# Attention with scaled, transposed probability rows, and the output weights loaded during it

## The chip, the cores and the metric

The kernel runs on one core of one Trainium2 chip. The metric is the device time in microseconds (us) from start to end of one execution; the median of three executions is compared. The engines are TensorE (PE; its weight loads are PEld), VectorE (DVE), ScalarE (ACT), GpSimd (POOL) and SyncE (SP), which here only issues DMAs.

## What is computed

One decoder layer on 1,024 tokens of width 1,024, everything in float32. The parts that matter here:

```
h = rmsnorm(x) * (1 + sc1) + sh1;  z = h @ w_in      # u, v, q, six k/v sets, gates
y_gm  = gelu(u) * (causal chunk mix of rmsnorm(gelu(v)) + b)
kc = gelu(flat(blocks(k_c) + pe_k) @ w1_k) @ w2_k    # 63 compressed keys; vc alike
for each head and branch b in (compressed, selected, window):
    s_b = q @ keys_b * scale - slope * distance;  p_b = masked_softmax(s_b)
    y += gate_b * (p_b @ values_b)
x = x + gt1 * (concat(y_gm, y_nsa) @ w_out)
h2 = rmsnorm(x) * (1 + sc2) + sh2
x = x + gt2 * moe(h2)        # top 4 of 32 experts;  out = rmsnorm(x)
```

There are 8 query heads of 64 dimensions in 2 key/value groups. A group's heads sit in one half of the 128 partitions, so a pair of heads (one of each group) is worked on side by side. With 16 blocks of 64 and the top 16 selected, the selected branch is full causal attention. The window is 512 keys.

## The kernel before

The program has five stages, one after the other; each ends when all engines have finished it, and the buffers of one stage are laid over those of an earlier one.

1. `project_tokens` (0 to about 375 us): the modulation vector and all projections, tile by tile of 128 tokens. The U and V weights are in `w_uv` (4 MB). When the last tile has used them, the first-layer compression weights (4 MB) are loaded into the same place (`s_cmpw`).
2. `attend` (375 to 871 us). First the compression: `compress` on TensorE multiplies the first-layer weights with the position rows (L676, one moving column per matmul) to get a bias, and then with the tokens (L683, 126 moving columns, weights stationary). The tokens `kk` are moved by eight ScalarE DMAs (L795, L796). TensorE's first wait is for the four small loads of position rows and second-layer weights (`s_w2`), issued at the start of the stage. Then the attention over eight query tiles `qt`, in the order that `attention_order` writes out and all engines follow:
   - `scores` (L713): negated queries times keys, a piece of up to 512 keys for the two groups at once, into one pair of PSUM banks `psA`. VectorE (`negate_scores`, L890) adds the distance term, writes the row to SBUF and takes its extreme. ScalarE (`exp_rows`, L814) takes the exponential of a whole branch of a row and sums it. These rows serve only for the sums.
   - `coefficients`, `parts_of_c`, `stage_c`: from sums, extremes and gates a logarithmic coefficient per row is made (`L840`, a Ln on ScalarE with table loads before and after it), split in three bf16 parts, transposed on TensorE (L724) and kept in `q_side` (L925).
   - `scores_of_keys` (L740, L750, L753): for each tile of 128 keys the scores are computed again, transposed, for all four heads of a group (512 columns), and masks, slopes and the coefficients are added by bf16 matmuls. ScalarE exponentiates the tile into `pT` (`exp_tile`, L824), and `weigh_values` (L769) multiplies it with the values into `psO`.
   Tiles of query tile `qt - 1` are interleaved with score pieces of `qt`; the tiles of the last one come alone (833 to 871 us). GpSimd does nothing here, and `keep_out` writes the result over the queries.
3. `route` (871 to about 1,120 us): `project` (L1137) multiplies a token tile with `w_out` (L1059 to L1062, issued when the stage starts), VectorE adds the residual (L1221, L1223), normalises, and picks experts; TensorE transposes and computes the logits in between. Before its first tile VectorE splits the expert biases into three bf16 parts (L1273 to L1286, seven operations on 3,072 columns).
4. `experts` (to about 2,750 us) and 5. `combine`.

Compression weights and tokens in use:

```
w1 = [w_uv[:, 4 * i:4 * i + 4, :].rearrange("p k (l h) -> p (k l) h", h=CMP_HIDDEN) for i in range(2)]
```

Of the kernel before, what the change touches and what calls it, by code (L numbers as in the profile page):

```python
# [79 lines left out]
def layer_kernel(nc, x, c, w_ada, b_ada, g_mix_norm, w_in, gm_w_s, gm_b_s, gm_norm_g, cmp_pe_k, cmp_w1_k, cmp_w2_k,  # L80
                 cmp_pe_v, cmp_w1_v, cmp_w2_v, w_out, g_ffn_norm, w_router, b_router, w_gate_up, b_gate_up, w_down,
                 b_down, g_final, k_ident, k_attn, k_attb, k_upper, k_expert, k_pairs, k_list,
                 k_quarter, out):
    ctx = ExitStack()
    with ctx:
# [22 lines left out]
        qT_all = stage3.enter_context(nc.sbuf_tensor("qT_all", [P, REP, SEQ], f32))  # L108
        stage2 = ExitStack()
        kT_all = stage2.enter_context(nc.sbuf_tensor("kT_all", [P, 4, SEQ], f32))  # L110
        misc = stage2.enter_context(nc.sbuf_tensor("misc", [P, TILES, MISC], f32))
        w_uv = stage2.enter_context(nc.sbuf_tensor("w_uv", [P, KD, 2 * GM_WIDTH], f32))

        with ExitStack() as s1:
            s_cmpw = project_tokens(nc, s1, sem, pb, x, c, w_ada, b_ada, g_mix_norm, g_ffn_norm, w_in, gm_w_s, gm_b_s,
                                    gm_norm_g, k_ident, (cmp_w1_k, cmp_w1_v), mod_d, ident, vec_t, mod_t, scale1, yT,
                                    qT_all, kT_all, misc, w_uv)
        with ExitStack() as s2:  # L118
            attend(nc, s2, sem, psum, s_cmpw, cmp_pe_k, cmp_w2_k, cmp_pe_v, cmp_w2_v, k_attn, k_attb, ident, qT_all,
                   kT_all, misc, w_uv)  # L120
        stage2.close()
        with ExitStack() as s3:
            route(nc, s3, sem, psum, x, w_out, g_ffn_norm, w_router, b_router, b_gate_up, b_down, k_upper, k_expert,
# [13 lines left out]
def project_tokens(nc, ctx, sem, pb, x, c, w_ada, b_ada, g_mix_norm, g_ffn_norm, w_in, gm_w_s, gm_b_s, gm_norm_g,  # L137
                   k_ident, cmp_w1, mod_d, ident, vec_t, mod_t, scale1, yT, qT_all, kT_all, misc, w_uv):
# [60 lines left out]
    def _(sp):  # L199
# [43 lines left out]

        sp.wait_ge(s_modrow, 1)
# [274 lines left out]
T_SLOPE_T = T_NEG + REP  # L519
T_SLOPE = T_SLOPE_T + TILES * 3 * HEADS  # L520
ATTN_COLS = T_SLOPE + 2 * HEADS
KSIDE = 2 * SEQ + NCP
B_MASK = KSIDE
B_CMASK = B_MASK + 4 * P
B_ID = B_CMASK + TILES * P
ATTB_COLS = B_ID + 2 * P
# [3 lines left out]
SIDE = 11  # L530
B_CMP, B_SLC, B_WIN = range(3)
KC, VC, KS, KW = range(4)

# [23 lines left out]
def key_tiles(qt):  # L557

    return ([(B_SLC, kt) for kt in range(qt + 1)] + [(B_WIN, kt) for kt in range(first_window_tile(qt), qt + 1)]
            + [(B_CMP, 0)])  # L560

def attention_order():
# [3 lines left out]
    for qt in range(TILES + 1):  # L567
# [5 lines left out]
        for n, piece in enumerate(pieces):  # L573
# [4 lines left out]
        order += head[done:]  # L578
# [6 lines left out]
def attend(nc, ctx, sem, psum, s_cmpw, pe_k, w2_k, pe_v, w2_v, k_attn, k_attb, ident, qT_all, kT_all, misc, w_uv):  # L585
# [7 lines left out]
    w2 = two("cmp_w2_", [P, M2, HD])  # L593
    pos = two("cmp_pos_", [L2, P])
# [3 lines left out]
    hid_b = sb("cmp_bias", [P, 2 * M2])  # L598
# [4 lines left out]
    tab_b = sb("attn_tables_b", [P, ATTB_COLS], bf16)  # L603
    ident_b = sb("ident_b", [P, P], bf16)
    gates = sb("gates", [P, TILES, NB])
    qn = two("q_negated", [P, REP, P])
    score = [[sb(f"scores{i}{g}", [P, S_COLS]) for g in range(2)] for i in range(2)]
    nmax = two("nmax", [P, NB])
    sums = two("sums", [P, NB])
    coef = sb("coef", [P, NB])  # L610
    lnc = sb("ln_coef", [P, NB])
    rest = sb("c_rest", [P, NB])
    c3 = two("c_parts", [P, HEADS, SIDE], bf16)
    qside = two("q_side", [P, REP * P], bf16)
# [1161 lines left out]
```

## Time and profile before

| | |
|---|---|
| time, median of 3 (lowest, highest) | 2781.54 us (2777.53, 2781.61) |
| profiled execution: time, span | 2778.26 us, 2776.6 us |
| mean granted TensorE clock | 0.921 of full |
| busy: PE, PEld | 2426.3 us (87%), 1424.1 us (51%) |
| busy: DVE, ACT, POOL | 865.1 us, 375.4 us, 716.7 us |

Stage times are read from the profiled execution, from its first instruction. PEclk is the share of the full clock (2.4 GHz) that was granted to TensorE in a stretch; 0.5 is its lower level, 1.2 GHz. A float32 matmul shows as two records; when the two halves of the array run side by side, records overlap, and the time of a group in the timeline is the span it covers.

### The profile page before, as it was taken

To read this page: it belongs to the slowest core of one execution; us is meant where nothing else is said; L and a number is where in the kernel's file an instruction comes from. 1 tells how busy PE (TensorE), PEld (TensorE's weight loads), DVE (VectorE), ACT (ScalarE), POOL (GpSimd) and SP (SyncE) were. 2 spreads that over 40 slices of the span, in tenths; PEclk is the share of its full clock that TensorE was granted. 3 is DMA by queue.
4 is the path that set the end of the run, shared out by engine and by line. 5 is a ranking of instruction groups with operands and counts; after the bars stand their busy time and mean duration, and the time that the engine had idled before them with its cause. 6 is when DMAs were issued, how large, how long until landed. Compare 5 with 4: busy or idle time off the path is not lost. (4 is left out here: it accounts for less than half of the span.)

```text
span 2776.6 us, 82328 instructions
## 1 busy us (share of the span) xinstructions
PE 2426.3 (87%) x33606; PEld 1424.1 (51%) x33606; DVE 865.1 (31%) x2946; ACT 375.4 (14%) x957; POOL 716.7 (26%) x1522
## 2 busy tenths in 40 slices
PE   5899977677786787499999899999999999999995
PEld 3677866222221344265655465555655555555552
DVE  2122212334330535132323233323333333333333
ACT  1000002545562001010000000000000000000001
POOL 1000000000000023333333333424334443444333
PEclk9999976679997887799999999999999999999997
DMA  9410040000003211838383938558589889899994
GB/s 324 156 69 31 1 122 0 1 0 1 1 1 102 89 58 53 308 98 313 97 308 102 360 118 319 198 211 298 187 316 376 295 298 356 295 358 392 377 385 144
DMA packets 176452, 522.05 MB, mean 188 GB/s; under 512 B 26728, under 2 KB 56064, under 8 KB 176160
## 3 DMA queue, kind: packets, MB, share of 16 engines
q1 hardware_dynamic: 141504, 476.68, 44.8%
q0 software_dynamic: 33824, 41.20, 7.3%
q10 hardware_dynamic: 976, 2.23, 0.3%
q8 instruction: 88, 1.44, 0.2%
q14 instruction: 60, 0.49, 0.0%
HBM read 487.21 MB, written 32.30 MB: 187 GB/s over the span
## 5 line engine op out<-in xcount | busy, mean ns | idle before, releaser
L1534 PE MATMUL psum<-w_ring,xT 128*32 128x256 f32 x18304 | 1038.7, 381 | 11.3 <-DMA w_ring<-in_w_gate_up 11.3
L1534 PEld LDWEIGHTS psum<-w_ring,xT 128*32 128x32 f32 x18304 | 586.1, 110 | 393.3 <-DMA w_ring<-in_w_gate_up 17.2
L1546 PE MATMUL psum<-w_ring,actT 128*32 128x256 f32 x9152 | 536.3, 385 | 25.2 <-DMA w_ring<-in_w_down 24.9
L1546 PEld LDWEIGHTS psum<-w_ring,actT 128*32 128x32 f32 x9152 | 285.1, 111 | 237.4 <-DVE actT L1601 35.5
L1468 POOL TENSOR_TENSOR scalars<-scalars 128x1 f32<-128x1 f32 x578 | 110.9, 192 | 823.5 <-DVE xT L1605 629.7
L1584 ACT ACTIVATE sig<-glu 128x128 f32<-128x128 f32 x286 | 88.9, 311 | 1515.8 <-DVE glu L1592 1515.8
L1592 DVE TENSOR_SCALAR glu<-psum 128x128 f32<-128x128 f32 x286 | 83.3, 291 | 626.9 <-PE psum L1534 620.2
L1487 POOL DMA_INDIRECT x_rows<-y_out,scalars_i x145 | 234.0, 1614 | 40.1 <-issue 39.8
L1614 DVE SCALAR_TENSOR_TENSOR y_out<-psum,scalars,gate_q 128x256 f32<-128x256 f32 x143 | 69.2, 484 | 435.6 <-DMA x_rows<-y_out,scalars_i 229.9
L1477 POOL DMA_INDIRECT x_gathered<-h_rows,scalars_i x144 | 153.0, 1062 | 82.6 <-issue 82.6
L713 PE MATMUL psum<-kT_all,q_negated 64*128 64x512 f32 (+3 forms) x384 | 101.3, 607 | 74.8 <-DVE nmax L890 74.2
L1094 POOL MEMSET eps_nhalf<- 128x1 f32 x1 | 0.1, 104 | 494.6 <-POOLq L118 494.6
L814 ACT ACTIVATE scores<-scores,nmax 128x64 f32<-128x64 f32 (+8 forms) x192 | 114.2, 599 | 75.6 <-DVE nmax L890 75.6
L890 DVE CUSTOM_DVE_ANT_0 scores<-psum,attn_tables 128x512 f32<-128x512 f32 (+4 forms) x192 | 82.3, 466 | 131.9 <-PE psum L713 131.7
L1527 PE MATMUL psum<-bias_parts,select 96*32 96x256 bf16 x1144 | 84.7, 278 | 35.2 <-DVE xT L1605 26.4
L713 PEld LDWEIGHTS psum<-kT_all,q_negated 64*128 64x128 f32 x384 | 36.6, 223 | 141.7 <-issue 134.9
L1137 PE MATMUL psum<-w_out_sb,yT 128*128 128x512 f32 x128 | 73.0, 723 | 38.3 <-DMA w_out_sb<-in_w_out 25.8
L824 ACT ACTIVATE probT<-psum 128x512 f32<-128x512 f32 (+1 forms) x148 | 80.1, 593 | 121.6 <-PE psum L753 57.5
L1601 DVE STREAM_TRANSPOSE actT<-lin 128x128 f32<-128x128 f32 x286 | 89.0, 311 | 9.9 <-DVE lin L1599 0.2
L1596 DVE SCALAR_TENSOR_TENSOR lin<-lin,glu 128x128 f32<-128x128 f32 x286 | 83.6, 292 | 9.9
L1599 DVE TENSOR_TENSOR lin<-lin,sig 128x128 f32<-128x128 f32 x286 | 83.5, 292 | 10.1 <-DVE lin L1596 0.4
L740 PE MATMUL psum<-qT_all,kT_all 64*128 64x512 f32 x264 | 82.9, 701 | 1.5 <-DVE q_side L925 1.5
(243 smaller groups left out, 2039.4 us busy)
## 6 DMA issues: line engine op xcount, KB each, us to landing
w_ring<-in_w_gate_up SPq DMA_DIRECT2D x256, 1024.0 KB, 9.8
w_ring<-in_w_down SPq DMA_DIRECT2D x128, 1024.0 KB, 19.4
ada<-in_w_ada SPq DMA_DIRECT2D x24, 1024.0 KB, 8.2
xt<-in_x SPq DMA_DIRECT2D x8, 512.0 KB, 6.9
w_uv<-in_w_in SPq DMA_DIRECT2D x4, 1024.0 KB, 12.6
x_rows_in<-in_x SPq DMA_DIRECT2D x8, 512.0 KB, 4.5
x_rows<-x SPq DMA_DIRECT2D x8, 512.0 KB, 2.9
h_rows<-h SPq DMA_DIRECT2D x8, 512.0 KB, 2.7
```

The lines of the kernel that those rows point to most:

```text
L713: last = nc.tensor.matmul(psA[g][:, col:col + m], qn[qt % 2][half(g), j, :], keys, start=True, stop=True)
L814: nc.scalar.activation(s, s, ACT.Exp, scale=-1.0, bias=nmax[qt % 2][:, col:col + 1], accum_out=sums[qt % 2][:, col:col + 1]).then_inc(s_ea, 1)
L1468: nc.gpsimd.tensor_tensor(tick[:], zero[:], zero[:], ALU.add).then_inc(s_steps, 1)
L1477: nc.gpsimd.indirect_dma_start(xg[:], None, h2_q, bass.IndirectOffsetOnAxis(ap=ids_x[:], axis=0), bounds_check=4 * (SEQ + BLK) - 1, oob_is ...
L1487: nc.gpsimd.indirect_dma_start(x1_q, bass.IndirectOffsetOnAxis(ap=ids_y[:], axis=0), y_out[:], None, compute_op=ALU.add).then_inc(s_ysc, 16)
L1527: nc.tensor.matmul(psU[h][j * BLK:(j + 1) * BLK, :], select[:, e:e + 1].to_broadcast([3 * E, BLK]), w_bias[:, j], start=True, stop=False)
L1534: last = nc.tensor.matmul(psU[h][j * BLK:(j + 1) * BLK, :], xT[:, k, :], w[:, j], start=False, stop=(k == KD - 1))
L1546: last = nc.tensor.matmul(psO[m * BLK:(m + 1) * BLK, :], actT[h][:, k, :], w[:, m * Q:(m + 1) * Q], start=False, stop=(h == 1 and k == KD ...
L1584: nc.scalar.activation(sig[:], glu[:], ACT.Sigmoid, scale=ALPHA).then_inc(s_sig[h], 1)
L1596: nc.vector.scalar_tensor_tensor(lin[h][:], lin[h][:], 1.0, glu[:], ALU.add, ALU.mult).then_inc(s_gated, 1)
L1599: nc.vector.tensor_tensor(lin[h][:], lin[h][:], sig[:], ALU.mult).then_inc(s_gated, 1)
L1601: nc.vector.transpose(actT[h][:].rearrange("p k q -> p (k q)"), lin[h][:]).then_inc(s_actT[h], 1)
```

## The change

Compression: the position rows are added to the tokens on VectorE (`kkp`), 8 operations; the tokens become the stationary side and the weights the moving one (256 columns), and the hidden rows are transposed on TensorE afterwards (4 transposes, 2 copies). The bias matmuls are gone. The small loads are issued in the stage before.

Attention: the unit is now one head pair of one query tile, 32 units `n`. The rows that ScalarE has exponentiated are kept: VectorE makes gate / sum per row (`coefficients`) and scales the selected branch in place; GpSimd scales the window and compressed branches. TensorE transposes the scaled rows in groups of up to two key tiles and two halves (`transpose_rows`, into `psT`); ScalarE copies a group to SBUF (`copy_group`; VectorE the last group of each unit); `weigh_values` takes 128 columns a pair. Groups follow their unit's scores two units later (`LAG`), so there are three score buffers. Score pieces alternate between two pairs of PSUM banks. The second computation of scores, the masks, the logarithm and the parts of c are gone, and with them the table `k_attb`.

Output weights: after the compression SP loads `w_out` into the place of `w_uv`, which now lives until routing ends. Routing takes them from there. Its first loads are the x tiles and the modulation rows, and the bias split is cut into six steps, one after each of the first six tiles.

```diff
+        w_uv = stage3.enter_context(nc.sbuf_tensor("w_uv_then_w_out", [P, KD, D], f32))
...
-        w_uv = stage2.enter_context(nc.sbuf_tensor("w_uv", [P, KD, 2 * GM_WIDTH], f32))
+        w2 = [stage2.enter_context(nc.sbuf_tensor(f"cmp_w2_{i}", [P, CMP_HIDDEN // P, HD], f32)) for i in range(2)]
...
+        for i in range(2):
+            sp.dma_start(pos[i][:], cmp_pe[i].rearrange("(l a) d -> l (a d)", a=2)).then_inc(s_cmpw, 16)
+            sp.dma_start(w2[i][:], cmp_w2[i].rearrange("(m p) d -> p m d", p=P)).then_inc(s_cmpw, 16)
...
+def branches(qt):
+    return [(B_SLC, 0, (qt + 1) * P), (B_WIN, WIN0, (qt + 1 - first_window_tile(qt)) * P), (B_CMP, CMP0, NCP)]
+def key_groups(qt):
+    tiles = [(B_SLC, kt, kt * P) for kt in range(qt + 1)]
+    first = first_window_tile(qt)
+    tiles += [(B_WIN, kt, WIN0 + (kt - first) * P) for kt in range(first, qt + 1)]
+    return [tiles[i:i + 2] for i in range(0, len(tiles), 2)] + [[(B_CMP, 0, CMP0)]]
...
-        pieces = [] if qt == TILES else [("scores", qt, j, n) for j in range(REP)
-                                         for n in range(len(score_pieces(qt)))]
-        tiles = [("tile", qt - 1, n) for n in range(len(key_tiles(qt - 1)))] if qt else []
-        head, tail = (tiles, []) if qt == TILES else (tiles[:-3], tiles[-3:])
+    for n in range(UNITS + LAG):
...
+        pieces = [("scores", n, i) for i in range(len(score_pieces(n // REP)))] if n < UNITS else []
+        m = n - LAG
+        groups = [("group", m, i) for i in range(len(key_groups(m // REP)))] if m >= 0 else []
         done = 0
...
-            upto = (n + 1) * len(head) // len(pieces)
-            order += head[done:upto]
+            upto = (i + 1) * len(groups) // len(pieces)
...
-        if qt < TILES:
-            for part in range(3):
-                order += tail[part:part + 1] + [("c", qt, part)]
+            if i == 1 and n:
+                order.append(("coef", n - 1, 0))
+        if n == UNITS:
+            order.append(("coef", n - 1, 0))
+        order += groups[done:]
     return order
...
+    psA = [[bank(0), bank(1)], [bank(2), bank(3)]]
+    psS = psA
+    psT = [bank(4), bank(5)]
...
+        wo = w_uv
+        sp.wait_ge(s_hps, 2)
+        sp.dma_start(wo[:, 0:KD // 2, :], w_out[0:GM_WIDTH, :].rearrange("(k p) n -> p k n", p=P)).then_inc(s_wo, 16)
+        for g in range(KV_GROUPS):
+            r0 = GM_WIDTH + g * REP * HD
+            sp.dma_start(wo[g * HD:(g + 1) * HD, KD // 2:KD, :],
+                         w_out[r0:r0 + REP * HD, :].rearrange("(j d) n -> d j n", d=HD)).then_inc(s_wo, 16)
...
+        for n in range(UNITS):
+            qt, j = divmod(n, REP)
+            pool.wait_ge(s_cf, 2 * n + 1)
+            for b, c0, m in branches(qt)[1:]:
+                for g in range(2):
+                    col = (g * REP + j) * 3 + b
+                    rows = score[n % (LAG + 1)][g][:, c0:c0 + m]
+                    nc.gpsimd.tensor_scalar(rows, rows, coef[qt % 2][:, col:col + 1], None, ALU.mult).then_inc(s_sl, 1)
...
+                for l in range(L2):
+                    if l % (L2 // 2) == 0:
+                        pe.wait_ge(s_cbsb, 1 + (2 * i + l // (L2 // 2) + 1) * KV_GROUPS)
+                    last = nc.tensor.matmul(psS[i][0][0:KV_GROUPS * N_CMP, 0:CMP_HIDDEN], kkp[i][:, l, :],
+                                            w1[i][:, l, :], start=(l == 0), stop=(l == L2 - 1))
+                last.then_inc(s_hps, 1)
...
-                    for l in range(L2):
-                        last = nc.tensor.matmul(psO[1][:, n:n + 1], w1[i][:, l, m * P:(m + 1) * P], posT[:, i, l:l + 1],
-                                                start=(l == 0), stop=(l == L2 - 1))
...
+                    last = nc.tensor.transpose(psS[i][1][:, m * P:m * P + KV_GROUPS * N_CMP],
+                                               hid_r[i][:, m * P:(m + 1) * P],
+                                               ident[0:KV_GROUPS * N_CMP, 0:KV_GROUPS * N_CMP])
...
-            if at:
-                pe.wait_ge(s_neg, at)
+            if at >= 2:
+                pe.wait_ge(s_neg, at - 1)
...
+        def transpose_rows(n, i):
+            at = g_no["group", n, i]
+            tiles = key_groups(n // REP)[i]
+            if tiles[0][0] == B_SLC:
+                pe.wait_ge(s_cf, 2 * n + 2)
+            if tiles[-1][0] != B_SLC:
+                pe.wait_ge(s_sl, 4 * n + (2 if tiles[-1][0] == B_WIN else 4))
+            if at >= 2:
+                wait_copied(pe, at - 2)
+            for t, (b, kt, c0) in enumerate(tiles):
+                m = NCP if b == B_CMP else P
+                for g in range(2):
+                    last = nc.tensor.transpose(psT[at % 2][0:m, (2 * t + g) * P:(2 * t + g + 1) * P],
+                                               score[n % (LAG + 1)][g][:, c0:c0 + m], ident[:])
+            last.then_inc(s_tp, 1)
...
+            at = g_no["group", n, i]
+            cols = 2 * P * len(key_groups(n // REP)[i])
+            act.wait_ge(s_tp, at + 1)
+            if at >= 4:
+                act.wait_ge(s_pv, at - 3)
+            nc.scalar.copy(pT[at % 4][:, 0:cols], psT[at % 2][:, 0:cols]).then_inc(s_pta, 1)
...
+                    nc.vector.tensor_tensor(kkp[i][:, a * L2 // 2:(a + 1) * L2 // 2, g * N_CMP:(g + 1) * N_CMP], lines,
+                                            bc_last(posT[:, i, a * L2 // 2:(a + 1) * L2 // 2], N_CMP), ALU.add
+                                            ).then_inc(s_cbsb, 1)
...
+        def coefficients(n):
+            qt, j = divmod(n, REP)
+            c = by_unit(coef[qt % 2], j)
+            dve.wait_ge(s_ea, 6 * n + 6)
+            if n >= 2 * REP:
+                dve.wait_ge(s_sl, 4 * (n - 2 * REP + 1))
+            ch.link(nc.vector.tensor_scalar(c, by_unit(sums[qt % 2], j), 1e-30, None, ALU.max))
+            ch.link(nc.vector.reciprocal(c, c))
+            nc.vector.tensor_tensor(c, c, gates[:, qt, :].rearrange("p (g j b) -> p g j b", g=2, b=3)[:, :, j, :],
+                                    ALU.mult).then_inc(s_cf, 1)
+            dve.wait_ge(s_cf, 2 * n + 1)
+            b, c0, m = branches(qt)[0]
             for g in range(2):
-                last = nc.vector.tensor_copy(qside[qt % 2][side(g), :], psO[qt % 2][side(g), :])
-            last.then_inc(s_qs, 1)
+                col = (g * REP + j) * 3 + b
+                rows = score[n % (LAG + 1)][g][:, c0:c0 + m]
+                last = nc.vector.tensor_scalar(rows, rows, coef[qt % 2][:, col:col + 1], None, ALU.mult)
...
     def _(sp):
+        for t in range(2):
+            sp.dma_start(xr[t][:], x_t[t]).then_inc(s_x[t], 16)
         sp.dma_start(gate1[:], mod_d[2 * D:3 * D].rearrange("(a n) -> a n", a=1).partition_broadcast(P)).then_inc(s_c, 16)
+        sp.dma_start(shift2[:], mod_d[3 * D:4 * D].rearrange("(a n) -> a n", a=1).partition_broadcast(P)).then_inc(s_c, 16)
+        sp.dma_start(scale2[:], mod_d[4 * D:5 * D].rearrange("(a n) -> a n", a=1).partition_broadcast(P)).then_inc(s_c, 16)
+        sp.dma_start(g2[:], g_ffn_norm.rearrange("(a n) -> a n", a=1).partition_broadcast(P)).then_inc(s_c, 16)
         for j in range(4):
             for i in range(2):
...
-        dve.wait_ge(s_b, 6 * 16)
-        nc.vector.tensor_copy(bias[:], b_rows[:]).then_inc(s_bias, 1)
...
+        def split_bias(step):
+            second, third = slice(E, 2 * E), slice(2 * E, 3 * E)
+            if step == 0:
+                dve.wait_ge(s_b, 6 * 16)
...
                 choose(t - 1, 1 - par)
+            if t < 6:
+                split_bias(t)
```

## Rows read from the trace of the kernel before

**Rows 1.** The page: span, and TensorE's granted clock in the 40 slices.

```profile
span 2776.6 us, 82328 instructions
PEclk9999976679997887799999999999999999999997
```

**Rows 2.** Windows: length, busy PE, PEld, DVE, ACT, POOL, PEclk, DMA share, GB/s.

```profile
394.00:421.00 27.00, 26.70 (x126) 26.73 (x126) 1.21 (x4) 0.00 (x0) 0.00 (x0) 0.50 0.04 15
421.00:451.00 30.00, 29.32 (x148) 27.79 (x148) 0.22 (x2) 2.57 (x5) 0.00 (x0) 0.94 0.00 1
451.00:597.00 146.00, 94.75 (x360) 34.84 (x362) 51.64 (x241) 71.09 (x224) 0.00 (x0) 0.61 0.00 1
597.00:710.00 113.00, 84.18 (x428) 27.72 (x428) 44.87 (x194) 63.26 (x151) 0.00 (x0) 0.97 0.00 1
710.00:833.00 123.00, 97.69 (x470) 31.22 (x468) 50.26 (x198) 70.94 (x157) 0.00 (x0) 0.94 0.00 1
833.00:871.00 38.00, 37.79 (x162) 9.31 (x158) 0.85 (x2) 15.18 (x28) 0.00 (x0) 0.96 0.00 1
871.00:897.00 26.00, 0.39 (x1) 0.40 (x2) 0.53 (x1) 0.00 (x0) 0.93 (x6) 0.58 0.81 214
897.00:926.00 29.00, 16.55 (x33) 6.73 (x32) 20.79 (x11) 0.06 (x1) 0.00 (x0) 0.74 0.42 128
```

**Rows 3.** Lines, 374 to 452 us: total busy, mean ns; idle before, releaser.

```profile
L676 PE MATMUL psum<-cmp_posT,w_uv 128*128 128x1 f32 x128 | 27.4, 352 | 0.4 <-DVE cmp_posT L847 0.4
L668 PE MATMUL psum<-ident,cmp_pos 16*128 16x16 f32 x1 | 0.3, 282 | 19.0 <-DMA cmp_w<-in_cmp_w_v 19.0
```

**Rows 4.** Who waited for whom in attention: total us, times, longest.

```profile
DVE scores L890 <- PE psum L713: 170.8, 104, 5.9
PE psum L713 <- DVE nmax L890: 91.7, 71, 2.6
```

**Rows 5.** The same columns by line and form, attention (451 to 871 us).

```profile
L824 ACT ACTIVATE probT<-psum 128x512 f32<-128x512 f32 x132 | 71.5, 594 | 120.0 <-PE psum L753 56.0 <-DVE nmax L890 47.8 <-issue 16.0
L890 DVE CUSTOM_DVE_ANT_0 scores<-psum,attn_tables 128x512 f32<-128x512 f32 x80 | 52.1, 689 | 84.9 <-PE psum L713 84.7
L753 PE MATMUL psum<-q_side,attn_tables_b 11*128 11x512 bf16 x132 | 27.5, 414 | 0.0
```

**Rows 6.** Timeline, TensorE at full clock: start, us, engine, line.

```profile
305.95 1.09 PE L395 MATMUL psum<-wsT,vn 128*64 128x128 f32 x16
306.98 1.09 PE L324 MATMUL psum<-ident,xt 128*128 128x128 f32 x8
...
355.22 3.94 PE L367 MATMUL psum<-w_misc,hT 128*128 128x280 f32 x16
...
867.85 1.94 PE L769 MATMUL psum<-probT,misc 128*64 128x512 f32 x8
```

**Rows 7.** VectorE and GpSimd at 22 us (timeline), and all of L436.

```profile
22.13 1.10 POOL L275 TENSOR_SCALAR_AFFINE_SELECT yT<-yT 128x1024 f32<-128x1024 f32 x1
22.21 1.57 DVE L436 TENSOR_SCALAR xt<-xt,rstd 128x1024 f32<-128x1024 f32 x1 [3.06 <-POOL rstd L268]
...
L436 DVE TENSOR_SCALAR xt<-xt,rstd x8: 743/745/1575, 18.4 to 292.1; 128x1024 f32<-128x1024 f32 x8
```

**Rows 8.** Timeline of the opening of routing.

```profile
896.61 6.60 PE L1137 MATMUL psum<-w_out_sb,yT 128*128 128x512 f32 x8 [25.82 <-DMA w_out_sb<-in_w_out]
904.85 1.76 DVE L1273 CAST bias_parts<-bias_rows 96x3072 bf16<-96x3072 f32 x1 [33.33 <-DMA bias_rows<-in_b_down]
925.96 5.58 PE L1137 MATMUL psum<-w_out_sb,yT 128*128 128x512 f32 x8 [12.45 <-DVE x L1223]
```

**Rows 9.** DMA issues: count, KB each, median us to landing.

```profile
cmp_in<-kT_all ACTq DMA_DIRECT2D x4, 256.0 KB, 10.6
...
g_ffn_rows<-in_g_ffn_norm SPq DMA_DIRECT2D x1, 512.0 KB, 23.4
upper<-k_upper POOLq DMA_DIRECT2D x1, 32.0 KB, 3.7
```

More of the change, by code:

```diff
@@ L518 @@
 T_NEG = DIST_C + TILES * NCP
[L519 to L526, printed above, removed]
+ATTN_COLS = T_NEG + REP
 WIN0 = SEQ
@@ L721, in transpose_c, with weigh_values @@
+        def weigh_values(n, i):
+            at = g_no["group", n, i]
+            qt, j = divmod(n, REP)
+            groups = key_groups(qt)
+            wait_copied(pe, at)
+            if i == 0 and j == 0 and qt >= 2:
                 pe.wait_ge(s_y, qt - 1)
-            for j in range(REP):
+            for t, (b, kt, c0) in enumerate(groups[i]):
                 for g in range(2):
-                    last = nc.tensor.matmul(psO[qt % 2][side(g), j * P:(j + 1) * P], c3[qt % 2][:, g * REP + j, :],
-                                            ident_b[:], start=True, stop=True)
@@ L757, in weigh_values @@
-        def weigh_values(qt, n):
-            at = t_no["tile", qt, n]
-            b, kt = key_tiles(qt)[n]
-            pe.wait_ge(s_et, 2 * at + 2)
-            if n == 0 and qt >= 2:
-                pe.wait_ge(s_y, qt - 1)
-            for g in range(2):
-                if b == B_CMP:
-                    v, p = vc[:, g * HD:(g + 1) * HD], pT[at % 3][g][0:NCP, :]
-                else:
-                    v = misc[:, kt, (b - B_SLC) * P + g * HD:(b - B_SLC) * P + (g + 1) * HD]
-                    p = pT[at % 3][g][:]
-                last = nc.tensor.matmul(psO[qt % 2][half(g), :], v, p, start=(n == 0),
-                                        stop=(n == len(key_tiles(qt)) - 1))
+                    c = slice((2 * t + g) * P, (2 * t + g + 1) * P)
@@ L771, in weigh_values @@
+                    if b == B_CMP:
+                        v, p = vc[:, g * HD:(g + 1) * HD], pT[at % 4][0:NCP, c]
+                    else:
+                        v, p = misc[:, kt, (b - B_SLC) * P + g * HD:(b - B_SLC) * P + (g + 1) * HD], pT[at % 4][:, c]
+                    last = nc.tensor.matmul(psO[qt % 2][half(g), j * P:(j + 1) * P], v, p, start=(i == 0 and t == 0),
+                                            stop=(i == len(groups) - 1))
             last.then_inc(s_pv, 1)
@@ L868, in _, with negate_scores @@
         ch.link(nc.vector.reciprocal(gates[:], gates[:]))
-        users = {}
-        def negate_scores(qt, j, n):
-            at = a_no["scores", qt, j, n]
+        def negate_scores(n, i):
+            qt, j = divmod(n, REP)
+            at = a_no["scores", n, i]
             dve.wait_ge(s_sc, at + 1)
-            pieces = score_pieces(qt)[n]
             col = 0
-            for b, s0, k0, m, d0, ends in pieces:
+            for b, s0, k0, m, d0, ends in score_pieces(qt)[i]:
+                again = any(b == e[0] for piece in score_pieces(qt)[:i] for e in piece)
+                if again:
+                    dve.wait_ge(s_neg, at)
```

346 lines of the change are left out of this document (118 added, 228 removed).

## The prediction

> **What bounds the kernel now.** The slices of the page come first [rows 1]: TensorE is busy nearly throughout, but between 370 and 600 us it holds a half clock for long, and near 880 us there is a dip. The windows show where the change acts [rows 2]: the compression (394 to 451 us), the attention (451 to 871), and the opening of the routing stage (871 to 926). In compression TensorE is busy all the time and is the bound. In attention no engine is saturated before 833 us: of the 382 us up to there TensorE is busy 276.6, ScalarE 205.3, VectorE 146.8. The table of waits says why [rows 4]: VectorE waits 170.8 us for score matmuls, and TensorE 91.7 us for the score maxima. One PSUM pair takes every score piece, so matmul and maximum take turns. At the opening of routing TensorE waits 25.8 us for the output weights and 12.5 us for the first residual row [rows 8]. Everything after routing (experts, combine) is the same code on the same buffers; I price it at nothing.
>
> **Compression: 39 us less.** TensorE now waits 19.0 us for the small second-layer weights, to 393.5 us, and then spends 27.4 us on 128 records with one moving column [rows 3]; 27.8 us of real compression follow (window 421 to 451) [rows 2]. The change loads the small tensors earlier and adds the position rows to the moved tokens on VectorE: 8 adds of 504 columns, by the 512-column VectorE form 0.69 us each [rows 5]. TensorE then waits for the moved tokens, which land 10.6 us after issue [rows 9] from about 376 us, and for two adds: a start at 391. The remaining six adds lie under its matmuls. It issues 32 matmuls of 256 columns, 64 records. The nearest form, 280 columns, took 3.94 us for 16, 0.246 each at full clock [rows 6], twice that at 1.2 GHz. In the routing stage the clock took some 6 us of work to rise from its lower level (the first eight records took 6.60 us) [rows 8]; I take 11 records at 0.49 and 53 at 0.246, 18.5 us, to 409.5. Activation, four extra transposes, two copies and the second layer add 3 us: 412.5 against 451.4. Gain 39. Bounds: 26 (all at 1.2 GHz, 31.5 us) to 42.
>
> **Attention, work on each engine.** There are 74 key tiles over the eight query tiles, 32 units (query tile by head pair), 35,840 score columns for each half.
> TensorE: scores stay. Two 512-column pairs of halves took 1.94 us (L769) [rows 6], 1.9 ns a column: 68 us. Recomputing transposed scores, masks and the side rows (L740, L750, L753; the last alone 27.5 us [rows 5]) goes. In come 592 transposes; eight took 1.09 us (L324) [rows 6], 0.136 each: 80.5 us. Weighing values becomes 296 pairs of 128 columns; four such pairs (16 records) took 1.09 us (L395) [rows 6], 0.27 each: 80.5 us. Sum 229 us at full clock, where the four windows have 314.4 busy.
> ScalarE: 220.5 us busy before in the four windows [rows 2]. Out go 148 exponentials of 512 columns at 0.594 [rows 5], 88 us, and 16 table loads around the logarithm, some 20 us; in come 136 copies priced like the exponential, 81 us. Sum 193.
> VectorE: 147.6 us before. Out goes the work on the parts of c, some 23; in come 32 coefficient chains of about 0.7, the scaling of 36,864 selected columns at 0.745/1024 us [rows 7] plus 0.1 each for 64 instructions, 33 us, and 32 copies of 256 columns at about 0.4. Sum 193.
> GpSimd: was idle; now scales 34,816 columns in 128 instructions. Its only wide row is a 1,024-column select, 1.10 us [rows 7]: 1.08 ns a column plus about 0.2 each, 62 us. No multiply of that width is shown; below nothing it can't be.
>
> **Attention, the time.** TensorE is the largest, at 229. The score pieces now have two PSUM pairs, so a maximum runs beside the next matmul and the turn-taking of rows 4 ends. Groups are due two units after their scores. In a unit of the last query tile TensorE works 10.8 us (3.2 scores, 7.6 groups), while ScalarE's longest block between copies, two row exponentials, is some 2.4 us and TensorE has 4 to 5 us of work queued before it needs the next copy; so that block is covered. The first query tiles have short units (2.5 us of TensorE work) whose maxima, coefficients and scaling take VectorE 3 to 5 us; there VectorE and the hand-offs bound. I allow TensorE the busy share of its best overlapped stretch, 97.7 of 123 us, 0.79 [rows 2]: 229/0.79 is 290, plus 5 for the first two units, which have scores only: 295 against 420. Gain 125. Bounds: 250 (TensorE nearly full) and 370 (busy share 0.62, three engines of nearly equal load waiting in turns): gains 170 and 50.
> One contention is shown: a VectorE scaling of 1,024 columns took 1.57 us instead of 0.745 when it started under GpSimd's select, and ended 0.55 us after it [rows 7]. VectorE's scaling and GpSimd's start from the same coefficient, so each of the 64 scalings may wait for one of GpSimd's, up to 0.9 us: at most some 45 us on VectorE, which brings it to 238; it lies inside the range.
> By the Trainium skill ("SBUF — State Buffer", SBUF: two separate sides) the shared port pair is an exclusive lock held for the whole instruction, which is what that row looks like; the sum is the same with or without it.
>
> **Routing: 31 us less.** With the weights loaded under attention, TensorE's first wait is for the `upper` matrix, 3.7 us to landing [rows 9]: a start 5 us after attention's end, not 25.1 (871.5 to 896.6). One tile's projection keeps TensorE busy 17 us there, 0.39 and 16.55 in the last two windows [rows 2]: ready 22 us after the end. VectorE needs the 15 constant loads by then. They and the two x tiles, 3.1 MB, now lead the queue; at the 214 GB/s of 871 to 897 [rows 2] that is 14.5 us, so they are hidden. The bias split (1.75 to 3.35 us a piece, 17 in all, which began at 904.9 [rows 8]) no longer stands before the residual. Two residual operations, 2.5 us, give a second projection at 24.5 us after the end; now it comes at 54.5 (925.96). Gain 30, and 1 to 2 more because TensorE then has idled 2.6 us instead of 12.5 and may keep its clock. Each tile period has some 24 us of TensorE work with VectorE under half busy, so the six pieces, at most 3.5 us each, are covered; uncovered they would cost 17. Were some load late, g_ffn's 23.4 us [rows 9] would be the case: gain 26. Bounds 14 and 33. The 4 MB of output weights move under attention, where DMA is idle [rows 2].
>
> **Sum.** 39 + 125 + 31 = 195. The profiled execution took 2778.3 us, within 0.12% of the median 2781.5: 2778.3 - 195 = 2583 us.
>
> **Rivals.**
> A: the clock stays low in attention. For: over 394 to 421 us TensorE was busy all the time with one-column matmuls, and the granted clock stayed at its lower level, 1.2 GHz [rows 2, 3]; a third of the new work is transposes. Against: the other two thirds are ordinary matmuls, and with ordinary work of 74 to 79% busy it was granted 0.94 to 0.97 [rows 2]. At 1.2 GHz TensorE's 229 become up to 458: attention some 460, and with compression at 26 and routing at 29 the time is 2763; a clock of 0.75 gives some 350 and 2640. Chance of over 2670 by this: 0.14.
> The Trainium skill ("TensorE: Matmul & The Clock Gate", Part 4: PE-mode transpose) says that transpose work does not engage the full clock. By that rule time would be near rival A's; no row here shows transposes alone.
> B: the engines wait in turns. VectorE's coefficient waits for ScalarE's last exponential of the unit, ScalarE's copies wait for transposes, these for GpSimd. Attention 370 gives 2658. Near the upper bound; chance 0.12 for 2625 to 2670.
> C: slower than before. GpSimd's multiply is the bound: the gains outside (70) mean that attention would have to exceed 490 us, 14 ns for each of 34,816 columns, 13 times its select. Its power takes that much and more, but for another operation. At 15 ns attention takes 522 us and the time is 2810. Chance 0.03.
> D: the early weights save nothing, because other loads end last: route gain 14, 2600. Inside the range; chance 0.05.
> Forecast, 2540 to 2625: 0.66.
>
> **Range and chances.** 2540 to 2665 reaches to rival B's end and leaves out A and C; the cases inside it hold 0.83. Changes within 0.2% (5.6 us) count as none. Faster 0.95, same 0.01, slower 0.04.
>
> **What will show it.** Right: compression ends near 412; no one-column matmuls; attention spans some 295 with TensorE near 0.8 busy at a clock over 0.9; GpSimd's scalings near 0.9 us; the first output projection 5 us after attention. Wrong, if the granted clock in attention is near its lower level, a GpSimd scaling takes several us, or VectorE's coefficients wait long for ScalarE.

## The result and the profile after

The changed kernel takes 2558.9 us (2558.07 to 2561.45), the kernel before on the same chip 2779.5 us (2776.36 to 2781.61): a ratio of 0.9209, 95% interval 0.9193 to 0.9225. The gain is 220.6 us; 195 were predicted, and the time lies inside the range, 24 us under the predicted one. In the later groups of runs the kernel before took 2775.8 to 2776.9 us, some 3 us less than here, so a difference of under 4 us between two groups is not read as an effect.

The page of the changed kernel, to be held against [rows 1]:

```profile
span 2557.7 us, 83989 instructions
PEclk9899998999988769999999998999999999999997
```

Eight slices of the kernel before stood at 7 or less, now three do. Four windows (columns as in [rows 2]): compression, opening of the attention, its body, and a little more than one tile of the routing stage.

```profile
390.00:406.60 16.60, 15.28 (x80) 12.74 (x78) 5.63 (x10) 2.41 (x4) 0.00 (x0) 0.95 0.10 24
406.60:430.00 23.40, 20.51 (x132) 13.79 (x132) 17.58 (x100) 15.48 (x69) 8.83 (x17) 0.64 0.62 164
450.00:650.00 200.00, 200.00 (x1714) 118.15 (x1712) 141.21 (x514) 142.21 (x356) 101.53 (x88) 1.00 0.01 1
756.00:782.00 26.00, 22.08 (x63) 11.95 (x62) 14.56 (x36) 2.40 (x6) 5.85 (x8) 0.85 0.17 61
```

The third row is the one to learn from: TensorE is busy for 200.00 of 200.00 us at its full clock (2.4 GHz), and no other engine reaches three quarters. The timeline gives the borders of the stages:

```profile
387.76 15.96 PE L687 MATMUL psum<-w_uv_then_w_out,cmp_rows 128*126 128x256 f32 x64 [12.60 <-DVE cmp_rows L835]
...
406.62 0.71 PE L723 MATMUL psum<-kT_all,q_negated 64*128 64x128 f32 x8 [0.57 <-DVE v_cmp L853]
...
686.01 6.64 PE L1107 MATMUL psum<-w_uv_then_w_out,yT 128*128 128x512 f32 x8 [6.58 <-DMA upper<-k_upper]
...
705.69 5.35 PE L1107 MATMUL psum<-w_uv_then_w_out,yT 128*128 128x512 f32 x8 [2.74 <-DVE x L1193]
...
887.66 0.21 PE L1150 MATMUL psum<-total_b,ones 128*128 128x32 bf16 x1 [2.12 <-DVE pairs L1238]
```

The first score matmul starts at 406.6 us where it started at 451.4: **compression gave 44.8** (39 predicted). The last attention result is copied out at 680.2: the attention takes 273.5 us instead of 420.1, **146.5** (125 predicted). From there to the last count of the routing stage it is 207.5 us instead of 236.9: **29.4** (31 predicted). What follows, experts and combine, takes 1670.0 us after and 1668.2 before.

Who waited for whom in the attention (us in total, times, longest), against [rows 4]:

```profile
ACT probT L810 <- PE psum L741: 61.1, 90, 1.7
DVE scores L872 <- PE psum L723: 58.8, 71, 1.7
...
PE psum L723 <- DVE nmax L872: 2.7, 2, 2.1
```

The 91.7 us in which TensorE waited for score maxima are 2.7 now. The engines that wait are those with time to spare.

### The profile page after: what moved, and what is told of

Read it like the earlier page. It is cut to its first block and busy times, and to the rows that moved or that the text cites. A ratio compares the mean times of both kernels' runs of the same rounds, so it can differ in the third digit from the quotient of the medians.

```text
span 2557.7 us, 83989 instructions
## 1 busy us (share of the span) xinstructions
PE 2344.6 (92%) x34294; PEld 1436.6 (56%) x34294; DVE 911.8 (36%) x3040; ACT 346.2 (14%) x919; POOL 847.6 (33%) x1649
## 5 line engine op out<-in xcount | busy, mean ns | idle before, releaser
L1516 PE MATMUL psum<-w_ring,xT 128*32 128x256 f32 x18304 | 1040.4, 381 | 9.3 <-DMA w_ring<-in_w_gate_up 9.3
L1516 PEld LDWEIGHTS psum<-w_ring,xT 128*32 128x32 f32 x18304 | 583.0, 110 | 396.3 <-DMA w_ring<-in_w_gate_up 15.5
L675 POOL TENSOR_SCALAR scores<-scores,coef 128x64 f32<-128x64 f32 (+5 forms) x128 | 132.8, 1053 | 161.1 <-DVE coef L887 161.1
L801 ACT ACTIVATE scores<-scores,nmax 128x64 f32<-128x64 f32 (+8 forms) x192 | 114.4, 598 | 14.2 <-DVE nmax L872 13.8
L741 PE MATMUL psum<-ident,scores 128*128 128x128 f32 (+1 forms) x592 | 102.3, 291 | 0.5 <-DVE scores L894 0.2
L286 POOL TENSOR_TENSOR vms<-vms,eps 128x8 f32<-128x8 f32 x8 | 5.6, 703 | 274.8 <-DVE vms L487 274.8
L741 PEld LDWEIGHTS psum<-ident,scores 128*128 128x128 f32 (+1 forms) x592 | 60.6, 139 | 58.5 <-issue 49.6
L759 PE MATMUL psum<-probT,misc 128*64 128x128 f32 x1056 | 88.4, 288 | 0.0
L810 ACT COPY probT<-psum 128x512 f32<-128x512 f32 (+1 forms) x136 | 77.3, 569 | 66.2 <-PE psum L741 61.1
```

The source lines that it names most:

```text
L675: nc.gpsimd.tensor_scalar(rows, rows, coef[qt % 2][:, col:col + 1], None, ALU.mult).then_inc(s_sl, 1)
L741: last = nc.tensor.transpose(psT[at % 2][0:m, (2 * t + g) * P:(2 * t + g + 1) * P], score[n % (LAG + 1)][g][:, c0:c0 + m], ident[:])
L759: last = nc.tensor.matmul(psO[qt % 2][half(g), j * P:(j + 1) * P], v, p, start=(i == 0 and t == 0), stop=(i == len(groups) - 1))
L801: nc.scalar.activation(rows, rows, ACT.Exp, scale=-1.0, bias=nmax[qt % 2][:, col:col + 1], accum_out=sums[qt % 2][:, col:col + 1]).then_in ...
L1516: last = nc.tensor.matmul(psU[h][j * BLK:(j + 1) * BLK, :], xT[:, k, :], w[:, j], start=False, stop=(k == KD - 1))
```

## The experiments

Each kernel differs from the changed one (2558.9 us) by the edit shown, the last one from the pipelined version. A figure behind a plus sign is the distance to 2558.9 us. The two bursts were executed once each, the others at least four times.

**TensorE as the bound: every transpose twice.**

```
-                for g in range(2):
+                for g in [0, 1] * 2:
                     last = nc.tensor.transpose(psT[at % 2]...
```

> Every one of the 592 transposes of the attention is issued twice, into the same place; all else as in the changed kernel (2558.9 us). Theory, TensorE is the bound of the attention: the second set costs what the first does, 592 x 0.136 = 80 us, so 2635 to 2645. Rival 1, the hand-offs between engines set the pace and TensorE only looks full: under +30 us, to 2590. Rival 2, transposes do not hold the clock up (half of the records would be transposes now): granted clock in the attention under 0.9 and more than +120 us, over 2680.

Measured 2623.6 us, ratio 0.9443 [0.9427, 0.9459]: +64.7. Every added transpose appears in the time, 0.109 us each (64.7 / 592), at a granted clock of 1.00 from 430 to 700 us. That excludes both rivals; the price, which gave 2635 to 2645, was off. A group's transposes at 600 us, in this kernel and then in the changed one:

```profile
600.49 1.09 PE L741 MATMUL psum<-ident,scores 128*128 128x128 f32 x8
601.51 0.66 PE L759 MATMUL psum<-probT,misc 128*64 128x128 f32 x8
```

```profile
600.37 0.66 PE L741 MATMUL psum<-ident,scores 128*128 128x128 f32 x4
600.96 0.66 PE L759 MATMUL psum<-probT,misc 128*64 128x128 f32 x8
```

From start to next start eight take 1.02 us and four 0.59: 0.108 us for each further one and about 0.16 us for each group. I had priced all at 0.136, a mean over runs of eight.

**One PSUM pair for the scores again.**

```
-            if at >= 2:
-                pe.wait_ge(s_neg, at - 1)
+            if at >= 1:
+                pe.wait_ge(s_neg, at)
...
-                    last = nc.tensor.matmul(psA[at % 2][g][:, col:col + m], ...)
+                    last = nc.tensor.matmul(psA[0][g][:, col:col + m], ...)
```

> The score pieces take one PSUM pair again instead of two, with the wait for every maximum; the order of the work and all else as in the changed kernel (2558.9 us). Rival, the second pair is what ended the turn-taking of the kernel before: the 112 pieces wait for about 1.6 us of maxima each, the attention gets 90 to 180 us longer, 2650 to 2740. Theory, the order does it: between two pieces TensorE has one to three groups of some 1.2 us from the unit two before, which cover the maxima but for the first units; +5 to +15 us, 2564 to 2574.

Measured 2589.3 us, ratio 0.9313 [0.9288, 0.9338]: +30.4, between the two theories. The four executions spread widely, from 2579.5 to 2592.9 us, so the price is some 20 to 34 us; the profiled one is the second slowest. Two windows of this kernel:

```profile
430.00:440.00 10.00, 9.03 (x47) 5.42 (x48) 5.46 (x28) 5.01 (x18) 3.52 (x6) 0.50 0.01 2
...
450.00:650.00 200.00, 186.49 (x1569) 109.32 (x1567) 132.69 (x497) 132.85 (x346) 93.84 (x87) 1.00 0.01 1
```

```profile
PE psum L723 <- DVE nmax L872: 23.8, 44, 2.3
```

The first query tile is copied out 12.9 us later than in the changed kernel, because the short waits of the opening keep the clock at 0.50 beyond 440 us; the remaining 17 us are spread over the body, where TensorE now idles 7%. So the second pair is worth some 30 us. In the kernel before the clock stood at 0.61 for 146 us of the attention [rows 2]; here it is low for some 40 us only. The rest of the 146.5 us gained belongs to the lesser work and the new order, which no run separates.

**GpSimd scales one column.**

The edit is in GpSimd's loop; the kernel leaves out the scaling of all but the first column of each stretch.

```
-                    rows = score[n % (LAG + 1)][g][:, c0:c0 + m]
+                    rows = score[n % (LAG + 1)][g][:, c0:c0 + 1]
```

> GpSimd scales only the first column of each of its 128 row stretches (the scaling of the other window and compressed columns is left out), so its 133 us of work fall to some 20. Theory, GpSimd's work is hidden although it costs twice what I priced, and what it takes from VectorE is hidden too: within 2 us of 2558.9, while VectorE's scaling of 1,024 columns falls from 1.02 us to about 0.75. Rival, the scaling holds the transposes of the window groups back or slows the first units: 5 to 20 us faster.

The time of the whole, 2794.0 us, can't be used: with the scaling left out other tokens reach the experts (18,944 weight-ring matmul records at L1516, not 18,304). The stages before them can. The first score matmul comes at 406.8 us and the last count of the routing stage at 887.74, against 406.6 and 887.66: GpSimd's work costs the path nothing. Its price and VectorE's, changed kernel and then this one:

```profile
L675 POOL TENSOR_SCALAR scores<-scores,coef 128x640 f32<-128x640 f32 x32 | 67.4, 2115 | 88.3 <-DVE coef L887 88.3
L675 POOL TENSOR_SCALAR scores<-scores,coef 128x64 f32<-128x64 f32 x64 | 27.2, 438 | 0.0
...
L894 DVE TENSOR_SCALAR scores<-scores,coef 128x1024 f32<-128x1024 f32 x8 | 7.8, 1021 | 0.1
```

```profile
L675 POOL TENSOR_SCALAR scores<-scores,coef 128x1 f32<-128x1 f32 x128 | 51.0, 418 | 239.5 <-DVE coef L887 239.5
L894 DVE TENSOR_SCALAR scores<-scores,coef 128x1024 f32<-128x1024 f32 x8 | 5.8, 766 | 0.1
```

GpSimd takes 2.9 ns a column ((2115 - 438)/576) and about 0.25 us on top, and 0.42 us even for one column, so its work falls to 51 us and not to the 20 expected. VectorE pays 0.26 us on average for each 1,024-column scaling beside it, hidden too.

**Transposes and the clock: at a high clock.**

```
         compress()
+        for n in range(256):
+            nc.tensor.transpose(psT[n % 2][:, n // 2 % 4 * P:(n // 2 % 4 + 1) * P], ident[:], ident[:])
         compressed()
```

> Between the compression's matmuls and its second layer TensorE does 256 transposes of 128x128 of the identity, with nothing between them; their results are not used. By the changed kernel's row (0.136 us each at full clock) the burst takes 35 us and the time is about 2592 (+33, two microseconds lie under the activation), with the granted clock at 1.0 in it. By the rule that transpose work does not engage the full clock it would fall to the lower level within the burst: up to 70 us, up to +68, 2600 to 2627, and a granted clock of 0.5 to 0.8 in the windows of the burst.

Measured 2586.9 us in one execution, +28.0. The burst and a window inside it:

```profile
404.53 28.11 PE L766 MATMUL psum<-ident 128*128 128x128 f32 x256
```

```profile
425.00:430.00 5.00, 5.00 (x49) 5.00 (x47) 0.00 (x0) 0.00 (x0) 0.00 (x0) 1.00 0.00 0
```

After 20 us of transposes alone the clock is still at its full level, and one takes 0.110 us.

**Transposes and the clock: at a low clock.**

```
         pe.wait_ge(s_cc, 16)
+        for n in range(128):
+            nc.tensor.transpose(psX[n % 2][:, n // 2 % 4 * P:(n // 2 % 4 + 1) * P], ident[:], ident[:])
```

> At the opening of routing, after TensorE's wait of 6.6 us and at its lower clock, it does 128 transposes of 128x128 of the identity before the first projection; their results are not used. In the changed kernel the first eight matmuls there took 6.64 us and the next eight 3.60. Theory, transposes bring the clock up as matmuls do: the burst takes some 17 to 18 us (0.22 each for the first 6 us, then 0.110), and the projection's first eight matmuls take 3.6 to 3.7 us: about +14, 2573. By the rule that transposes do not engage the full clock: the burst takes 28 us at a granted clock of 0.5, and the first eight matmuls after it take 6.6 us again: +28, 2587.

Measured 2573.1 us in one execution, +14.2.

```profile
687.64 16.74 PE L1135 MATMUL psum<-ident 128*128 128x128 f32 x128 [7.15 <-DMA upper<-k_upper]
704.22 3.60 PE L1107 MATMUL psum<-w_uv_then_w_out,yT 128*128 128x512 f32 x8
```

```profile
686.00:690.00 4.00, 2.36 (x11) 2.39 (x12) 0.00 (x0) 0.00 (x0) 0.00 (x0) 0.50 0.89 319
690.00:694.00 4.00, 4.00 (x26) 4.00 (x25) 0.00 (x0) 0.00 (x0) 0.00 (x0) 0.63 1.01 290
694.00:698.00 4.00, 4.00 (x40) 4.00 (x38) 0.56 (x1) 0.00 (x0) 0.00 (x0) 1.00 1.01 211
```

The clock rises within the burst, and the projection after it starts at full clock: 3.60 us where the changed kernel needed 6.64. The rule of the Trainium skill ("TensorE: Matmul & The Clock Gate", Part 4: PE-mode transpose), that transposes do not engage the full clock, does not hold for these float32 transposes in either direction.

**The one-column matmuls put back.**

```
+            pe.wait_ge(s_cbsb, 1)
+            for i in range(2):
+                for m in range(M2):
+                    for l in range(L2):
+                        nc.tensor.matmul(psO[1][:, M2 * i + m:M2 * i + m + 1], w1[i][:, l, m * P:(m + 1) * P],
+                                         posT[:, i, l:l + 1], start=(l == 0), stop=(l == L2 - 1))
```

> The 128 one-column matmuls of the kernel before stand again between the transposed position rows and the compression; their result is not used. Theory: they run at the lower clock as before (27.4 us, 0.214 each); they start at about 375.5 us, 12.3 us of them lie under TensorE's wait for the moved tokens, so the compression starts at about 403 instead of 387.8: +14 to +17, 2573 to 2576. Rival 1, they cost their full 27 us: 2586. Rival 2, the clock is high when the loop before ends and stays so: 13.7 us, all but 1 to 2 us hidden, 2559 to 2561.

Measured 2569.7 us, ratio 0.9251 [0.9237, 0.9266]: +10.8, under the 14 to 17 expected; the profiled execution was the slowest of four (2574.0), and in it the compression starts at 403.73, as the theory said, and the first score matmul at 422.3 instead of 406.6. The one-column matmuls begin 2.3 us after the busy loop of the stage before has ended; between the two TensorE does two small transposes:

```profile
376.40 27.46 PE L687 MATMUL psum<-cmp_posT,w_uv_then_w_out 128*128 128x1 f32 x128 [0.28 <-DVE cmp_posT L834]
```

```profile
374.00:376.00 2.00, 0.22 (x4) 0.18 (x2) 1.38 (x2) 0.00 (x0) 0.18 (x2) 1.00 0.00 0
376.00:378.00 2.00, 1.72 (x10) 1.62 (x9) 0.19 (x1) 0.00 (x0) 0.10 (x1) 0.58 0.65 73
378.00:403.00 25.00, 25.00 (x119) 25.00 (x118) 8.06 (x9) 0.00 (x0) 0.00 (x0) 0.50 0.45 113
406.00:408.00 2.00, 2.00 (x8) 1.71 (x7) 0.00 (x0) 0.00 (x0) 0.00 (x0) 0.74 0.00 0
```

The clock fell to its lower level (1.2 GHz) just as they began, behind a stretch in which TensorE was nearly idle, and the gap may be the reason. What the run shows is that 27 us of one-column matmuls without a gap did not bring it back, while the 256-column matmuls behind them, from 403.73, did so within 4 us. Of their 27.5 us some 12 lie under the wait for the moved tokens.

**The small loads late.** Position rows and second-layer weights are loaded at the start of the compression, ahead of the tables, on the same queue as before.

> The position rows and the second-layer weights are loaded at the start of the compression again, not in the loop before. In the kernel before TensorE waited 19.0 us for them. Now the position rows stand ahead of VectorE's adds: loads done at about 393.5 as before, then a copy and two adds (2.5 us) before the first matmul of the compression, at 396 to 397 instead of 387.8: +8 to +9.5, 2567 to 2568. Rival, only the position rows count and they land early: within 2 us of 2558.9.

Measured 2554.3 us, ratio 0.9198 [0.9184, 0.9212], not slower: my theory fell. TensorE waits for the small loads until 380.3 us, which lies under its wait for the moved tokens: the compression starts at 385.4. In this kernel, and then in the kernel before:

```profile
cmp_w<-in_cmp_w_k SPq DMA_DIRECT2D x1, 64.0 KB, 3.3
cmp_w<-in_cmp_w_v SPq DMA_DIRECT2D x1, 64.0 KB, 5.4
```

```profile
attn_tables_b<-k_attb POOLq DMA_DIRECT2D x1, 976.0 KB, 10.8
...
cmp_w<-in_cmp_w_k SPq DMA_DIRECT2D x1, 64.0 KB, 12.2
cmp_w<-in_cmp_w_v SPq DMA_DIRECT2D x1, 64.0 KB, 15.9
```

The same loads land in 5.4 us from the same place. What has gone from the queues beside them is the 976 KB table of the recomputed scores, so its removal, and not the earlier issue, most likely made them land before the tokens; the table was not put back alone to show it. The 19.0 us wait of [rows 3] has not gone as a whole: in the changed kernel TensorE waits 12.6 us for the tokens and their adds.

**The opening of routing, its two parts apart.** The first kernel loads the output weights behind the constants of that stage, the second runs the six pieces of the bias split ahead of the first residual row, the third does both.

```
-        sp.wait_ge(s_hps, 2)
-        sp.dma_start(wo[:, 0:KD // 2, :], w_out[0:GM_WIDTH, :]...).then_inc(s_wo, 16)
...
         sp.dma_start(token[:], k_pairs).then_inc(s_c, 16)
+        sp.dma_start(wo[:, 0:KD // 2, :], w_out[0:GM_WIDTH, :]...).then_inc(s_w, 16)
...
```

```
+        for step in range(6):
+            split_bias(step)
         dve.wait_ge(s_c, 16 * 15)
...
-            if t < 6:
-                split_bias(t)
```

> The 4 MB of output weights are loaded at the opening of routing again, behind the constants and ahead of the biases, as the kernel before had it but for the x rows; the bias split stays spread. Theory: TensorE waits some 25 us again instead of 6.6, then runs on: +18 to +22, 2577 to 2581. Rival, the two parts of the routing edit give their gains only together (the residual row waits for the other in either case): under +10.

> The six pieces of the bias split stand ahead of the first residual row again; the output weights still load under the attention. The bias rows follow the constants in the queue, which are complete 16 us after the attention's end; the biases land perhaps 4 us later, the split takes some 17 us by the rows of before, so the first residual comes at about 38 to 42 us after the end instead of 23: +12 to +17, 2571 to 2576. Rival, the split is hidden under the projection (22 us): within 2 us of 2558.9.

> Both at once: weights loaded late and bias split ahead, the opening of routing much as before the change. Theory, the two lie one beside the other (the split needs the biases, which now queue behind the weights, and runs while TensorE projects): +27 to +31, less than the sum of the two single runs (30 to 39). Rival, additive: the sum of the two single runs within 2 us.

Measured 2583.2 us (0.9300 [0.9284, 0.9315], +24.3), 2575.7 (0.9273 [0.9257, 0.9288], +16.8) and 2589.4 (0.9327 [0.9312, 0.9343], +30.5). The first costs 2 us more than expected, the other two lie within what was expected. The sum of the single ones is 41.1, so 10.6 us are shared. From the attention's end to the last count of the routing stage the traces give +23.8, +16.5 and +33.0, so 7.3 shared; the additive rival is out by either. In the first, TensorE starts at 714.04 after 32.60 us of waiting, since the weights queue behind all that now leads. With both late, the split runs while TensorE projects, as the theory said:

```profile
710.13 5.73 PE L1105 MATMUL psum<-w_uv_then_w_out,yT 128*128 128x512 f32 x8 [32.05 <-DMA w_uv_then_w_out<-in_w_out]
714.55 1.75 DVE L1245 CAST bias_parts<-bias_rows 96x3072 bf16<-96x3072 f32 x1 [35.74 <-DMA bias_rows<-in_b_down]
733.06 1.29 DVE L1189 TENSOR_TENSOR x<-psum,gate 128x512 f32<-128x512 f32 x2
```

**A faster version: the projection pipelined.** Each tile of the routing stage of the changed kernel has this gap:

```profile
774.04 3.62 PE L1121 MATMUL psum<-w_router_sb,h2T 128*128 128x32 f32 x16 [3.92 <-ACT h2T L1166]
777.47 5.29 PE L1107 MATMUL psum<-w_uv_then_w_out,yT 128*128 128x512 f32 x8
```

TensorE waits 3.92 us for ScalarE's copies, and the next sixteen and eight records run partly at the lower clock. My version takes the PSUM pair by the tile's parity, projects one half of the columns at a time, and issues the next tile's first half in `logits`, between its transposes and its matmuls. The wait for `upper` stands in `places`.

```
+    psO, psX = ((bank(0), bank(1)), (bank(2), bank(3))), (bank(4), bank(5))
...
-        def project(t, par):
-            pe.wait_ge(s_x1, t)
+        def project(t, n):
+            if t >= 2:
+                pe.wait_ge(s_x1, t - 1)
...
             last.then_inc(s_xps, 1)
+            if t + 2 < TILES:
+                project(t + 2, 0)
```

> A version of my own: the output projection gets two PSUM pairs, and its first half for the next tile is issued between the transposes and the router matmuls of a tile; the wait for the upper matrix stands before its first use. In the changed kernel TensorE waits 3.9 us in each tile for the copies of the transposed rows and its clock then falls (the next group of eight matmuls takes 5.3 us, not 3.6). Theory, TensorE bounds routing and both losses go: 5 us for each of 7 tiles plus 5 at the opening, 30 to 45 us faster than 2558.9, 2514 to 2529. Rival, the chain through VectorE and GpSimd from residual to list takes over: under 10 us faster.

Measured 2504.4 us, ratio 0.9019 [0.9004, 0.9034]: 54.5 us faster than the changed kernel, where 30 to 45 were expected.

```profile
756.00:782.00 26.00, 26.00 (x96) 13.89 (x94) 19.61 (x47) 4.51 (x10) 9.45 (x12) 1.00 0.31 108
```

```profile
764.63 1.87 PE L1125 MATMUL psum<-w_router_sb,h2T 128*128 128x32 f32 x16
766.34 3.68 PE L1108 MATMUL psum<-w_uv_then_w_out,yT 128*128 128x512 f32 x8
```

TensorE is busy throughout at full clock; the router's sixteen records take 1.87 us instead of 3.62, which my sum had missed. From one tile's router matmuls to the next it is 16.5 us (748.15 to 764.63), as against 23.9 (750.13 to 774.04). The 7.4 us between them are the wait of 3.92, 1.75 on the router's records and 1.61 on the projection's first eight.

**The short gaps filled.**

```
+        def fill(count):
+            for n in range(count):
+                nc.tensor.transpose(psT[n % 2][:, 0:P], ident[:], ident[:])
...
+            fill(5)
             pe.wait_ge(s_hT, 2)
...
+            fill(6)
             pe.wait_ge(s_cmp, 1)
...
             if at >= 2:
+                fill({2: 18, 3: 4, 4: 4, 5: 6}.get(at, 0))
                 pe.wait_ge(s_neg, at - 1)
```

> On top of the version with the pipelined projection (2504.4 us): 46 transposes of the identity, not used, stand in TensorE's short waits between the compression and the second unit of the attention, where the clock fell to its lower level from 408 to 425 us after gaps of 0.3 to 2.1 us. Theory, the gaps make the clock fall: it stays at 1.0 there, and the stretch of 17 us at 0.5 gets 4 to 8 us shorter, 2496 to 2501. Rival, VectorE and ScalarE bound these short units, so only TensorE's busy time falls: within 2 us of 2504.4, or 1 to 3 us slower for the added transposes.

Measured 2499.4 us, ratio 0.9000 [0.8987, 0.9012], against 0.9019 [0.9004, 0.9034]: the intervals overlap. The trace says more. The same 17 us with the pipelined projection alone, and then here:

```profile
408.00:425.00 17.00, 15.35 (x84) 10.46 (x84) 12.49 (x80) 12.29 (x56) 6.79 (x13) 0.50 0.76 180
```

```profile
408.00:425.00 17.00, 15.87 (x152) 11.80 (x148) 14.03 (x83) 12.02 (x57) 6.79 (x13) 1.00 0.92 244
```

The clock reads 1.00 from 404 to 430 us, and the stretch from the first score matmul to the last copy of the attention is 269.4 us instead of 273.5 with the pipelined projection alone, 4.1 shorter. The gaps did make the clock fall; the gain in the whole is not separated from the spread.

## Why the prediction was right, and where it was off

**Compression (39 predicted, 44.8).** Right in mechanism except for one step: "the change loads the small tensors earlier" has no effect, as the late loads showed. The start came at 387.8 and not 391, since the stage before ended a little earlier and the first moved tokens landed at 385.8. The 64 records took 15.96 us and not 18.5. The clock rose from its lower level, as I had taken it, somewhat sooner than after the 5.4 us I had allowed:

```profile
388.00:390.00 2.00, 2.00 (x5) 1.60 (x6) 1.54 (x3) 0.00 (x0) 0.00 (x0) 0.50 0.18 45
390.00:392.00 2.00, 2.00 (x7) 1.62 (x6) 2.00 (x3) 0.00 (x0) 0.00 (x0) 0.60 0.00 0
392.00:394.00 2.00, 2.00 (x11) 1.75 (x10) 2.00 (x3) 0.00 (x0) 0.00 (x0) 1.00 0.00 0
```

It reads 0.50 for the first 4 us and 1.00 from 392 on. What was too high was the price of a record: with some 9 of them in the first 3.8 us (my estimate), the other 55 took 0.22 us each, not the 0.246 of the 280-column form. The adds cost 0.93 us each from start to start instead of 0.69.

**Attention (125 predicted, 146.5).** Two terms were off in opposite directions. TensorE's work was mis-sized: a unit of the last query tile takes 12.47 us (636.82 to 649.29), not 10.8, since short groups pay their 0.16 us each time; 229 scaled by 12.47/10.8 is 264. The busy share was mis-sized more: 0.79 was read from a kernel in which engines took turns, and the body has 1.00. Scaled work of 264 and some 8 us lost to the low clock of the opening (my estimate: half of 17 us at 0.50) make up nearly all of the 273.5. Rivals A and B were told apart by the clock (1.00) and by the doubled transposes (all of them paid). Rival C had the direction right: the multiply costs 2.9 ns a column and not the 1.08 of the select, GpSimd's work 133 us and not 62. It stays under 273, far from the 490 at which it would decide. The contention with VectorE, priced at up to 0.9 us for each scaling, is smaller. Nor is it a wait for GpSimd's whole instruction, as the prediction had read the row of [rows 7]; in a unit of the last query tile:

```profile
643.22 2.47 POOL L675 TENSOR_SCALAR scores<-scores,coef 128x640 f32<-128x640 f32 x1 [7.31 <-DVE coef L887]
643.83 1.28 DVE L894 TENSOR_SCALAR scores<-scores,coef 128x1024 f32<-128x1024 f32 x1
```

VectorE's second scaling starts and ends while GpSimd's instruction runs; it takes 1.28 us where 0.77 is its time alone, and GpSimd's next one, without VectorE beside it, takes 1.88 instead of 2.47. Both are slowed, and neither is held to the other's end. The Trainium skill ("GPSIMD Engine Reference", 4.1 Engine selection) calls one-input work there roughly line-rate; this tensor-scalar multiply took 2.9 ns a column, and VectorE's with none beside it 0.75 (766 ns for 1,024), so the trace does not bear that out.

**Routing (31 predicted, 29.4).** The steps came as written: TensorE starts 5.8 us after the attention's end (5 predicted), the constants are complete at 696.1, before the first projection is done at 702.9, and the second projection starts 25.5 us after the end (24.5 predicted). Undoing both parts costs 30.5. Rival D, other loads ending last, is out by the start at 5.8 us. The hope that TensorE keeps its clock over the short wait was not met: the eight first records took 6.64 us, and the next tile's 5.35.

**Nothing else** changed by more than the 1.8 us of the experts' stage. The time came out inside the range with two terms of the attention wrong in opposite directions, so its nearness to the forecast is partly luck: with 264 us of work and the share of 0.79 the attention comes to 339, and the sum to 2627.

## What to carry to other kernels

When one engine becomes the bound, sum its work at full rate from rows of the same group length, and allow it the busy share of the new order: a share read from a kernel in which engines take turns is a property of the turns. A short wait of TensorE can cost more than its length, when the clock falls behind it: look for work of the next tile to put there, as the pipelined projection did for 54 us. Not every run of waits does that: in the body of the kernel with one PSUM pair TensorE idled 7% and the clock stayed at 1.00. Before a load is moved, look at what lands beside it: a load removed elsewhere may already make it early enough.

## What the runs showed of the hardware

- 128 one-column matmuls, back to back, ran at a granted clock of 0.50 for 27 us without bringing it up. 256 transposes of 128 columns in a row held it at 1.00, and 128 of them begun at 0.50 brought it to 1.00 within 8 us.
- Behind waits of 0.3 to 2.1 us between 404 and 410 us it fell to 0.50 until 425 us, and 46 transposes in the gaps of that opening kept it at 1.00.
- GpSimd's multiply by a per-row scalar: 0.42 us for one column, 2.9 ns for each further one at widths of 64 to 640; VectorE's 1,024-column scaling beside it took 1.02 us on average instead of 0.77, and one ran wholly within a GpSimd instruction.
